# Merge, output product and queries as one stage; cross attention by query tiles; GpSimd takes the remainder of the merged rows

## The reference, cut to what matters

```python
merged = sum(gates[:, :, n] * (o @ w_branch[l, n]) for n, o in enumerate((oA, oB, oC)))
x = x + merged @ w_out[l]
x = x + cross_attn(rmsnorm(x, norm_x[l]), mk, mv, w_xq[l], w_xo[l])
f, ffn_buf = conv_ffn(rmsnorm(x, norm_ffn[l]), w_up[l], ffn_conv_w[l], w_down[l], ffn_buf)
```

## Time and profile before

| | |
|---|---|
| median of three runs | 2914.32 us (2913.46 to 2923.27) |
| profiled execution | 2914.09 us, span 2912.4 us |
| TensorE busy | 2653.1 us, 91% of the span |
| VectorE / ScalarE / GpSimd busy | 53% / 33% / 10% |
| mean granted TensorE clock | 0.946 |
| merge's first to query product's last matmul | 1323.6 to 1749.6 us |
| cross attention, TensorE's work | 1753.9 to 1936.0 us |
| feed-forward, from its first matmul | 1947.6 us on |

### The profile page before, as it was taken

The page is one execution under the profiler, slowest core; times in us unless marked ns, Lnnn a source line. Parts: engine busy times, 40 slices in busy tenths (PEclk is TensorE's granted clock), DMA queues, the critical chain, the costliest instruction groups (busy, mean ns, idle before and its releaser), DMA issues. The chain is left out here.

```text
span 2912.4 us, 49232 instructions
## 1 busy us (share of the span) xinstructions
PE 2653.1 (91%) x20376; PEld 2485.5 (85%) x20376; DVE 1552.3 (53%) x2381; ACT 970.6 (33%) x1486; POOL 304.4 (10%) x600
## 2 busy tenths in 40 slices
PE   8999789587999999967979897879999999999998
PEld 6999666476999999957979696879999999999997
DVE  5565357574344445443642501417873688558863
ACT  4332165222222232221110411225443454335542
POOL 0011124100000000000000001002111211113321
PEclk9999899787999999988989998869999999999999
DMA  3222356544223222215471117243344433453343
GB/s 145 62 78 77 124 185 224 155 132 125 90 89 95 84 84 81 83 61 189 139 264 41 74 70 289 67 173 123 126 127 146 159 128 126 141 169 124 130 124 100
DMA packets 194434, 364.29 MB, mean 125 GB/s; under 512 B 43488, under 2 KB 129120, under 8 KB 191264
## 3 DMA queue, kind: packets, MB, share of 16 engines
q1 hardware_dynamic: 174112, 316.48, 33.3%
q0 software_dynamic: 9600, 35.40, 3.4%
q10 hardware_dynamic: 10512, 9.44, 0.9%
HBM read 277.21 MB, written 84.95 MB: 124 GB/s over the span
## 5 line engine op out<-in xcount | busy, mean ns | idle before, releaser
L2729 PE MATMUL ffn_bank<-ffn_x_hi,ffn_w_hi 128*128 128x384 f32 x1248 | 422.4, 338 | 24.9 <-DVE ffn_x_lo L3005 15.4
L2729 PE MATMUL ffn_bank<-ffn_x_lo,ffn_w_hi 128*128 128x384 f32 x1248 | 419.4, 336 | 0.0
L2729 PE MATMUL ffn_bank<-ffn_x_hi,ffn_w_lo 128*128 128x384 f32 x1248 | 419.4, 336 | 0.0
L2719 DVE TENSOR_TENSOR ffn_w_lo<-ffn_w_raw,ffn_w_hi 128x1024 fp32r<-128x1024 f32 (+1 forms) x228 | 272.7, 1196 | 232.4 <-ACT ffn_w_hi L2712 232.4
L2712 ACT CAST ffn_w_hi<-ffn_w_raw 128x1024 fp32r<-128x1024 f32 (+1 forms) x228 | 234.9, 1030 | 431.1 <-PE ffn_bank L2729 390.0
L2729 PEld LDWEIGHTS ffn_bank<-ffn_x_hi,ffn_w_hi 128*128 128x128 f32 x1248 | 236.4, 189 | 28.6 <-DVE ffn_w_lo L2719 11.7
L2729 PEld LDWEIGHTS ffn_bank<-ffn_x_hi,ffn_w_lo 128*128 128x128 f32 x1248 | 236.4, 189 | 0.7
L2729 PEld LDWEIGHTS ffn_bank<-ffn_x_lo,ffn_w_hi 128*128 128x128 f32 x1248 | 236.1, 189 | 0.0
L378 PE MATMUL delta_dense<-x_hi,win_win_hi 128*128 128x384 f32 x576 | 216.1, 375 | 9.5 <-PEq L109 5.7
L378 PE MATMUL delta_dense<-x_lo,win_win_hi 128*128 128x384 f32 x576 | 197.0, 342 | 0.0
L378 PE MATMUL delta_dense<-x_hi,win_win_lo 128*128 128x384 f32 x576 | 196.8, 342 | 0.0
(11 more groups left out here) (395 smaller groups left out, 5682.3 us busy)
## 6 DMA issues: line engine op xcount, KB each, us to landing
ffn_w_raw<-in_w_up SPq DMA_DIRECT2D x132, 512.0 KB, 3.3
win_win_raw<-in_w_in SPq DMA_DIRECT2D x52, 512.0 KB, 3.7
ffn_w_raw<-in_w_down SPq DMA_DIRECT2D x48, 512.0 KB, 3.5
scratch_gates<-delta_gates SPq DMA_DIRECT2D x72, 192.0 KB, 3.9
merge_gate<-scratch_gates POOLq DMA_DIRECT2D x24, 576.0 KB, 4.2
ffn_w_raw<-in_w_xo SPq DMA_DIRECT2D x24, 512.0 KB, 3.3
scratch_features<-prepare_a_r_b_k POOLq DMA_DIRECT2D x12, 768.0 KB, 4.3
ffn_w_raw<-in_w_down SPq DMA_DIRECT2D x24, 384.0 KB, 3.1
```

The costliest lines, as they stand in the source:

```text
L2719: dve.tensor_tensor(self.lo[s][:, 0:kt], self.raw[s][:, 0:kt], self.hi[s][:, 0:kt].bitcast(F32), ALU.subtract).then_inc(self.rest, 1)
L2729: mm = pe.matmul(bank, w[s][:, k, :], x, start=(start and k == 0 and i == 0), stop=(stop and k == kt - 1 and i == 2), skip_group_check=True)
```

## The change

`Product`, `Norm`, `StreamSplit`, `stage_merge`, `stage_residual` and `stage_queries` go. `stage_mix` takes their place: one stage with 120 units in one order (branches 0 and 1 by turns, then branch 2, then the output product, then the queries), seven banks in a ring, and all traffic in pieces of 128 x 384 (192 KB) on SyncE's queue. Weights have one raw buffer and two split ones. The sum of branches 0 and 1 goes to DRAM (`partial`) and comes back for branch 2. The merged rows never leave SBUF: ScalarE rounds them, GpSimd subtracts. The norm's factor is no longer applied to the operand but to the query's bank, so the query product starts on the unnormalised rows. `xt2` is stored row by row.

`stage_cross` loads its queries in tiles of 128 tokens (512 KB), the memory keys and values itself, and turns the values in step 1. It writes the first three tiles of its result straight into the feed-forward's operand, and loads and splits the first three weight tiles of the feed-forward, whose buffers now live in a stage around both. `Weights` is the feed-forward's class, made general. The diff, cut:

```diff
+class Weights:
...
+    def __init__(self, st, tag, tiles, raws, splits, uses):
+        self.tiles, self.raws, self.splits, self.uses = tiles, raws, splits, uses
+        make = lambda n, count, dt: [st.sb(f"{tag}_{n}{s}", [P, KD, P], dt) for s in range(count)]
+        self.raw, self.hi, self.lo = make("raw", raws, F32), make("hi", splits, F32R), make("lo", splits, F32R)
...
+    def load(self, eng, j):
...
+        src, kt = self.tiles[j]
+        if j >= self.raws:
+            eng.wait_ge(self.rest, j - self.raws + 1)
+        eng.dma_start(self.raw[j % self.raws][:, 0:kt], src).then_inc(self.arrived[j % self.raws], 16)
...
+    def split_hi(self, act, j):
...
+        act.wait_ge(self.arrived[j % self.raws], 16 * (j // self.raws + 1))
+        if j >= self.splits:
+            act.wait_ge(self.done, self.uses * (j - self.splits + 1))
+        act.copy(self.hi[j % self.splits][:, 0:kt], self.raw[j % self.raws][:, 0:kt]).then_inc(self.rounded, 1)
...
+def stage_mix(nc, env, io):
...
+        NBK = 7
...
+        order = [(kind, f) for f in range(KD) for kind in (0, 1)] + [(2, f) for f in range(KD)] + \
+            [("out", f) for f in range(KD)] + [("q", f) for f in range(KD)]
+        units = [(kind, f, c) for kind, f in order for c in range(NTC)]
...
+        W = Weights(st, "w", [weight(kind, f) for kind, f in order], 1, 2, NTC)
+        R1, R2 = (sb(f"operand{i}", [P, 2 * KD, T], F32R) for i in range(2))
+        INS, OUTS_, RAWS = 5, 3, 6
+        pieces = sb("pieces", [P, INS + OUTS_ + 3 + RAWS, TC])
+        ins, outs = (lambda i: pieces[:, i % INS]), (lambda o: pieces[:, INS + o % OUTS_])
+        tmp, raw = (lambda i: pieces[:, INS + OUTS_ + i % 3]), (lambda r: pieces[:, INS + OUTS_ + 3 + r % RAWS])
...
+        for kind, f, c in units:
+            if kind in (0, 1, 2):
+                piece_of[kind, f, c] = len(incoming)
+                incoming.append(("gate", kind * KD + f, c))
+            if kind == 2:
+                incoming.append(("partial", f, c))
...
+        operand_of = {0: lambda k: (R1[:, k], R1[:, KM + k]), 1: lambda k: (R1[:, 2 * KM + k], R1[:, 3 * KM + k]),
+                      2: lambda k: (R2[:, k], R2[:, KM + k]), "out": lambda k: (R1[:, k], R1[:, KD + k]), "q": lambda k: (R2[:, k], R2[:, KD + k])}
+        branch_no = lambda br, c, k: br * NTC * KM + c * KM + k
+        branch = [(br, c, k) for br in range(3) for c in range(NTC) for k in range(KM)]
+        SPLIT_AT = {-1: branch[0:4], 0: branch[4:8], 1: branch[8:12], 2: branch[12:16], 3: branch[16:20], 4: branch[20:24]}
+        SPLIT_AT |= {6 + i: branch[24 + i:25 + i] for i in range(NTC * KM)}
...
+                def load_branch(br, c, k):
...
+                    if r >= RAWS:
+                        sp.wait_ge(S("branch_rest"), r - RAWS + 1)
+                    sp.dma_start(raw(r), io["branch"][br, :, k, cols(c)]).then_inc(S(f"branch_in{r % RAWS}"), 16)
...
+                def load_piece(i):
...
+                    if i >= INS:
+                        sp.wait_ge(S("taken"), i - INS + 1)
...
+                    sp.dma_start(ins(i), src).then_inc(S(f"piece_in{i % INS}"), 16)
...
+                W.load(sp, 0)
+                for b in branch[0:6]:
+                    load_branch(*b)
+                W.load(sp, 1)
+                for b in branch[6:12]:
+                    load_branch(*b)
...
+                for n in range(N + 2):
+                    if n >= 2 and units[n - 2][0] in (1, "out", "q"):
+                        store(*units[n - 2])
+                    through = max((piece_of[u] + (u[0] == 2) + 1 for u in units[:max(n, 0)] if u in piece_of), default=0)
+                    while loaded < min(len(incoming), through + INS):
+                        load_piece(loaded)
+                        loaded += 1
+                    if n < N and n % NTC == 0:
+                        W.load(sp, n // NTC + 2)
+                    for b in branch[12 + 4 * n:16 + 4 * n] if n < 3 else branch[20 + n:21 + n]:
+                        if n < 3 or n >= 4:
+                            load_branch(*b)
...
+                for f in range(KD):
+                    for c in range(NTC):
+                        pool.wait_ge(S("merged_rounded"), row(f, c) + 1)
+                        pool.tensor_tensor(R1[:, KD + f, cols(c)], tmp(c), R1[:, f, cols(c)].bitcast(F32), ALU.subtract).then_inc(S("merged_rest"), 1)
...
+                    if f == 0:
+                        pool.tensor_copy(sumsq(c), sq(i)).then_inc(S("added"), 1)
+                    else:
+                        pool.wait_ge(S("added"), i - 2)
+                        pool.tensor_tensor(sumsq(c), sumsq(c), sq(i), ALU.add).then_inc(S("added"), 1)
...
+                def merged_hi(f, c):
+                    act.wait_ge(S("taken"), piece_of[2, f, c] + 2)
+                    if f == 0 and c == 0:
+                        act.wait_ge(W.done, at[2, 0, 0])
+                    act.copy(R1[:, f, cols(c)], tmp(c)).then_inc(S("merged_rounded"), 1)
...
+                def output_row(f, c):
...
+                    act.activation(R2[:, f, cols(c)], outs(o), ACT.Copy, scale=V("norm_x", f)).then_inc(S("x_rounded"), 1)
+                    if i >= 3:
+                        act.wait_ge(S("added"), i - 2)
+                    act.activation(sq(i), outs(o), ACT.Square).then_inc(S("squared"), 1)
...
+                def root(c):
+                    act.wait_ge(S("summed"), c + 1)
+                    act.activation(rs(c), SUMS[:, 0:TC], ACT.Sqrt, scale=1.0 / D, bias=env["eps"][:, 0:1]).then_inc(S("root"), 1)
...
+                for n in range(N + 1):
+                    if n < N and n % NTC == 0:
+                        W.split_hi(act, n // NTC + 1)
+                    for b in SPLIT_AT.get(n, []):
+                        branch_hi(*b)
...
+                def branch_lo(br, c, k):
...
+                    dve.wait_ge(S("branch_rounded"), r + 1)
+                    hi, lo = operand_of[br](k)
+                    tt(lo[:, cols(c)], raw(r), hi[:, cols(c)].bitcast(F32), ALU.subtract).then_inc(S("branch_rest"), 1)
...
+                def empty(n):
+                    kind, f, c = units[n]
+                    dve.wait_ge(W.done, n + 1)
...
+                        if f == 0:
+                            dve.wait_ge(S("root"), c + 1)
+                            dve.reciprocal(rs(c), rs(c)).then_inc(S("inverse"), 1)
+                            dve.wait_ge(S("inverse"), c + 1)
...
+                        tt(outs(o), dense(n), rs(c), ALU.mult).then_inc(S("q"), 1)
...
+                    if kind == 0:
+                        if f:
+                            dve.wait_ge(S("partial"), row(f - 1, c) + 1)
+                        tt(tmp(c), dense(n), ins(i), ALU.mult).then_inc(S("taken"), 1)
+                    elif kind == 1:
+                        o = out_no(kind, f, c)
+                        free_out(o)
+                        tt(outs(o), dense(n), ins(i), ALU.mult).then_inc(S("taken"), 1)
+                        dve.wait_ge(S("taken"), i + 1)
+                        tt(outs(o), outs(o), tmp(c), ALU.add).then_inc(S("partial"), 1)
...
+                    elif kind == 2:
+                        if f:
+                            dve.wait_ge(S("merged_rest"), row(f - 1, c) + 1)
...
+                        tt(tmp(c), dense(n), ins(i), ALU.mult).then_inc(S("taken"), 1)
+                        taken(i + 1)
+                        dve.wait_ge(S("taken"), i + 1)
+                        tt(tmp(c), tmp(c), ins(i + 1), ALU.add).then_inc(S("taken"), 1)
...
+                        tt(outs(o), dense(n), ins(i), ALU.add).then_inc(S("taken"), 1)
...
+                def operand_lo(n):
...
+                        stt(out=R2[:, KD + f, cols(c)], in0=outs(out_no(kind, f, c)), scalar=V("norm_x", f), in1=R2[:, f, cols(c)].bitcast(F32),
...
+                    if n < N and n % NTC == 0:
+                        W.split_lo(dve, n // NTC + 1)
...
+                def sums(c):
...
+                    pe.wait_ge(S("added"), (KD - 1) * NTC + c + 1)
...
+                    if n >= NBK:
+                        emptied(pe, n - NBK)
...
+                                       2: ("branch_rest", lambda k: branch_no(2, c, k)), "out": ("merged_rest", lambda k: row(k, c)),
+                                       "q": ("x_rest", lambda k: row(k, c))}[kind]
+                        before = lambda k: pe.wait_ge(S(name), count(k) + 1)
+                    operand = lambda k: tuple(x[:, cols(c)] for x in operand_of[kind](k))
+                    W.multiply(pe, n // NTC, dense(n), operand, 0, True, True, before)
...
     with Stage(nc, "cross") as st:
...
-        kv, ident = env["kv"], env["mask"]("ident")
-        q = st.sb("q", [P, KD, T])
+        kv, ident = st.sb("kv", [P, 2 * KD, NMEM]), st.sb("ident", [P, P])[:]
+        q = [st.sb(f"q{i}", [P, KD, P]) for i in range(3)]
+        W, E = env["ffn_weights"], env["ffn_operands"]
...
-                def load_q(c):
```

(69 more changed lines are left out.)

680 lines of the change are left out of this document (223 added, 457 removed).

## The result

The changed kernel takes 2820.76 us (median of four runs, 2819.65 to 2823.99) against 2913.89 us beside it: ratio 0.9675, interval 0.9654 to 0.9697. Two more series of the same kernel gave 2826.21 (2823.84 to 2828.81, ratio 0.9682, 0.9654 to 0.9711) and 2817.94 (2809.76 to 2822.4, six runs, 0.9662, 0.9637 to 0.9687). The forecast was 2825.

A forecast was written before the change was run, and what follows sets the result against it. TensorE, busy 91% of the span, bounds the kernel with its work plus holes, 105 us of them from merge to queries. 2914.1 - 67.8 - 10 - 11.7 + 0.7 = 2825.3, so 2825 us predicted; range 2808 to 2850.

The forecast's parts named there:

- First matmul of the merged stage: Start of the merged stage: first issue stays at 1311.0, first weight tile usable from 1313.8, first matmul at 1315.8.
- Seventh unit: Merged stage's start: after 24 pieces done at 1337.5, unit 7 starts at 1338 instead of 1345.8, gain 7.8 us.
- From there to the last query matmul: Merged stage from unit 7: 137.8 + 200.6 + 2.9 + 2.5 us, queries ending at 1681.8 instead of 1749.6.
- the 2.5 us for the clock: Merged stage: allowance for clock 0.81 having to recover, estimated between nothing and 8.1 us.
- the forecast's sign: Profile after: from the seventh unit to the last query matmul about 344 us, clock 1.00, no idle over a microsecond.
- Covered work: Merged stage: remainders (GpSimd subtraction 1.36 us), norm, `xt2` stores, residual loads and VectorE's branch 2 work cost nothing.
- Small rings: Merged stage: weights' loop 5.6 of 6.27 us, pieces' loop 4.4 to 5.7 of 5.2; both fit narrowly, cost 0.
- rival 1: Branch part: a small ring or the port sets the pace, +5 to +28 us, most likely 2838; chance 0.22.
- Rival 3: Branch 2: pieces do not overlap in the one queue, +113 us, 2938, slower than before; chance 0.03.
- Cross attention: Up to tile 0: TensorE starts 10.5 us after queries, tile 0 weighed at +50.7 instead of +62.8; gain 10.
- Rival 2: Cross attention gains nothing because 1 MB of keys every 3.5 us asks for 300 GB/s: 2835; chance 0.09.
- Feed-forward: Its start: first matmul at 5.4 instead of 11.6 us, gain 6.2; first 54 matmuls gain 5.5; outer stage costs 0.7.

The follow-up runs named there:

- best: Changed kernel with two raw weight buffers, first two gates and ScalarE's branch pieces moved ahead, memory keys loaded head by head: 2816.14 us, ratio 0.9666.
- after_again: The changed kernel run again unchanged, as reference for its variants: 2826.21 us, ratio 0.9682.
- after_five: The changed kernel a third time, unchanged, for comparison with two raw buffers: 2817.94 us over six runs, ratio 0.9662.
- raw2: Changed kernel with two raw weight buffers in the merged stage instead of one: 2815.13 us, ratio 0.9661.
- xt2_again: Changed kernel plus a 4.6 MB DRAM-to-DRAM copy of `xt2` ahead of the cross attention's first keys: 2835.0 us, ratio 0.9732.
- before_again: The kernel before the change, run and traced a second time unchanged: 2915.62 us in one run.
- before_third: The kernel before the change, run and traced a third time unchanged: 2928.39 us in one run.
- ffn_own: Changed kernel, but the feed-forward again loads and splits its own first 24 pieces and three weight tiles: 2832.35 us, ratio 0.9716.

## Why the prediction was right

By the means of three traces of each kernel the merged stage gives 68.9 us (457.4 - 388.5), the cross attention up to tile 0 gives 12.4 (62.8 - 50.4) and after it 0.8, the feed-forward 9.4 (977.4 - 968.0), and the stages ahead 4.3. Together 95.8, the difference of the mean spans. The forecast had 67.8, 10, nothing, and 11.7 - 0.7 = 11.0: 88.8. The 4.3 us of the stages ahead, which the change leaves alone, count as luck, and no term of the sum stands for them.

- **First matmul of the merged stage.** Forecast 22.1 us after the stage before, measured 21.8 to 22.0 in every trace.
- **Seventh unit.** Forecast 44.3 us after the stage before; it came at 1335.9, 48.8, and at 46.7 and 48.5 in the two further traces. This term of the sum was mis-sized. I followed ScalarE's and VectorE's order and let a piece land in 3.4 us, whenever asked. But the pieces of branches 0 and 1 go through six slots of their own, and this loop I did not work out. The tile `mix_pieces` in the stretch 1304 to 1336, with what its engines' idle time waited for, puts a number on it:

```profile
L2134 SPq DMA_DIRECT2D mix_pieces<-scratch_branch x26: 319/430/2171, 1304.7 to 1334.4; - x26
...
L2249 DVE TENSOR_TENSOR mix_operand<-mix_pieces,mix_operand x24: 548/555/559, 1308.3 to 1333.0; 128x384 fp32r<-128x384 f32 x24
...
  DMA mix_pieces<-scratch_branch: 11.0, 7
  ACT mix_operand L2202: 6.6, 5
  DMA mix_pieces<-scratch_gates: 2.8, 1
...
DMA to landing us min/median/max: 2.3/4.0/4.8
```

  Seven waits for branch pieces, 11.0 us, at landings of 4.0. The gates, which I held for the worst, cost one wait of 2.8. The 24th piece is split at 1333.6, 46.5 after the stage before, where I had 43.8. How much of this the six slots cost is not shown: the longest of the seven waits, 5.4 us, is for pieces that SyncE issued only behind the five gates and a weight tile, and one issue took SyncE up to 2.2 us (first row). No run has more slots for branch pieces; best, which changes only the order and the weights' buffers, has the 24th split at 43.8. Of the 2.3 us from there to the seventh unit, 1.4 are the half clock: in this trace the sixth unit takes 3.5 us, in after_again, at full clock, 2.1.
- **From there to the last query matmul.** Forecast 343.8, measured 340.0 (341.5 and 339.9 in the other two). That is the usual 0.174 us a matmul and the sums, with the wait at the 19th unit; the 2.5 us for the clock were not needed, since full clock was back before the seventh unit here and in after_again, and 1.9 us behind its start in after_five. The start's 4.5 us too many and these 3.8 too few nearly cancel, so the stage's total came out right in part by compensation. The wait of 1.7 us in after_again also breaks the forecast's sign that no idle time over a microsecond would be left there.
- **Covered work.** GpSimd's subtraction took 1.05 us in the mean, not 1.36; VectorE's additions 0.58, nearly without the 0.76 us that I had priced for a wait beside GpSimd. These are the groups of the merged stage by form, VectorE's additions and then GpSimd's subtractions:

```profile
L2292 DVE TENSOR_TENSOR mix_pieces<-mix_pieces 128x384 f32<-128x384 f32 x24 | 13.9, 579 | 3.5 <-DMA mix_pieces<-scratch_partial 1.1
```

```profile
L2185 POOL TENSOR_TENSOR mix_operand<-mix_pieces,mix_operand 128x384 fp32r<-128x384 f32 x24 | 25.3, 1053 | 763.3 <-ACT mix_operand L2208 763.3
```

- **Small rings** (rival 1). Not the pace, as forecast, and with more room than the margins of 0.7 and 0.5 us (the one buffer for weights costs its 1 or 2 us, as raw2 shows): the DMA issues have landings of 3.0 and 3.1 where I had reckoned with 3.4 to 4.7, and 3.9 for weights.

```profile
mix_pieces<-scratch_gates SPq DMA_DIRECT2D x72, 192.0 KB, 3.1
cross_k_sample<-in_mem_k SPq DMA_DIRECT2D x8, 1024.0 KB, 6.7
...
mix_w_raw<-in_w_branch SPq DMA_DIRECT2D x24, 256.0 KB, 3.0
...
mix_pieces<-scratch_partial SPq DMA_DIRECT2D x24, 192.0 KB, 3.0
```

  Rival 3, pieces one at a time, falls by the same rows: at 216 GB/s a 192 KB piece would have to land in 0.9 us if only one were under way.
- **Cross attention.** First matmul forecast 10.5 us after the queries, measured 11.2; tile 0 forecast at 50.7, measured 50.0 to 50.6. I took 10 of the 12 us that this gives, for keys that might come late; they did not, though 1 MB took 6.7 us instead of 5.6, because the groups and the turning ahead of them left room. Rival 2 did not come about. xt2_again shows what late keys cost, 13.6 us in one wait, but there they stand behind a copy, and their own pace was not put to the test.
- **Feed-forward.** Forecast 6.2 and 5.5, less 0.7 for the outer stage. The wait fell by 5.9 to 5.67 us; the first 54 matmuls took 10.9 us instead of 17.4, so 6.5; from the last matmul to the end of the span pass 12.1 us instead of 11.7, so the outer stage costs 0.4. That makes 12.0, and the profiled pair shows 8.8. Of the 3.2 given back, 2.7 lie in two waits for late weights (3.55 and 5.90 us against 2.59 and 4.12). Part of this is spread between executions: before_again waits 2.98 and 5.67 there, before_third 3.92 and 3.98. But the second of these waits is 5.1 to 6.4 us in all eleven traces of changed kernels and 4.6 in the mean of the three before, so that the change costs a microsecond there is not excluded. It would not be the preload's doing, since ffn_own has 5.6 too. ffn_own, +11.5, confirms the term.
- **Ahead of the change.** Forecast nothing, and 6.6 us less in the profiled pair, where the windowed attention alone has 7.5 less (157.4 against 164.9). Two more traces of before brought 159.8 and 160.7, inside the 154.7 to 164.4 of the eleven traces of changed kernels. The three of before average 161.8, the eleven 158.4. That the pair's 6.6 us are the change's work is not shown, and a small part of them is not excluded.

## What to carry to other kernels

When one stage drains, stores, meets a barrier and loads, take the price from the first matmuls' waits on either side, not from the busy shares; here the merged stage as a whole was worth 69 us, of which the norm's place made 10, and the engine chosen for a remainder nothing. For a ring, ask how much slack its consumer has and how many full banks lie between it and TensorE before calling it the pace; and at a start, where nothing has run up a lead yet, work out each ring's loop with landings under load, also that of the smallest pieces. Measure edits of a few us in their own stretch, with the kernel before traced more than once.
